# Gate GEMMs as one block of eight pairs with seven block products for eight, other jobs in the SWA stage, GpSimd rotation by tiles

## What is computed

```
h   = RMSNorm(x)
z   = h @ w_in          # q latent 384 | kv latent 256 | rope key 32 | SWA q 512 | SWA k 128 | SWA v 128 | gates 2048
A   = multi-head latent attention, 8 heads, chunk-causal (64-frame chunks)
B   = sliding-window attention, 8 heads on 2 kv heads, this chunk and two before, learned sinks
m   = sum_b sigmoid(gate_b) * (branch_b @ w_branch[b])
x   = x + RMSNorm(m @ w_out)
x   = x + RMSNorm(SwiGLU(RMSNorm(x)))
```

## Time and profile before

| | us |
|---|---|
| median of three runs | 902.55 (902.31 to 903.01) |
| the profiled execution, own time | 903.12 |
| its span, first to last instruction | 901.3 |
| TensorE busy in the span | 885.1 |
| VectorE busy | 491.9 |
| ScalarE busy | 385.4 |
| GpSimd busy | 75.7 |

### The profile page before, as it was taken

The page is one execution under the profiler, slowest core; times in us unless marked ns, Lnnn a source line. Parts: engine busy times, 40 slices in busy tenths (PEclk is TensorE's granted clock), DMA queues, the critical chain, the costliest instruction groups (busy, mean ns, idle before and its releaser), DMA issues.

```text
span 901.3 us, 13817 instructions
## 1 busy us (share of the span) xinstructions
PE 885.1 (98%) x5513; PEld 804.0 (89%) x5513; DVE 491.9 (55%) x758; ACT 385.4 (43%) x769; POOL 75.7 (8%) x73
## 2 busy tenths in 40 slices
PE   8999999999999998999999999999999999999997
PEld 7888999999976877998789999999999998888886
DVE  5523532433354565564779877777777774343124
ACT  5211422335453555452666545444445443332112
POOL 0300197140030000000000000000000000000000
PEclk9999999999999999999999999999999999999999
DMA  7623245153330001654612233332233326222202
GB/s 271 176 78 93 69 128 179 57 158 92 100 71 1 2 1 36 205 181 181 193 72 81 83 93 95 94 87 76 73 94 94 94 84 242 72 72 93 71 24 117
DMA packets 101599, 91.97 MB, mean 102 GB/s; under 512 B 8496, under 2 KB 85312, under 8 KB 101392
## 3 DMA queue, kind: packets, MB, share of 16 engines
q1 hardware_dynamic: 95216, 86.19, 30.9%
q10 hardware_dynamic: 5424, 2.99, 1.1%
q0 software_dynamic: 896, 1.92, 0.7%
HBM read 79.60 MB, written 12.40 MB: 102 GB/s over the span
## 4 chain that ended last, share of the span: by engine, by line
PE 90%; DVE 5%; ACT 4%; issue 1%; DMA 0%; DVEq 0%; POOL 0%; ACTq 0%; POOLq 0%
PE ps L1180 26%; PE ps L1181 25%; PE ps L1182 25%; PE ps L1362 2%; PE ps L1411 1%; PE ps L1373 1%; PE ps L1235 1%; PE ps L1458 1%; PE ps L1332 1%; PE ps L1405 1%; PE ps L1336 1%; ACT probs L897 1%; PE ps L1433 1%; PE ps L1443 1%; DVE nm_c L1735 1%
## 5 line engine op out<-in xcount | busy, mean ns | idle before, releaser
L1671 DVE TENSOR_TENSOR wlo<-raw,whi 128x1024 fp32r<-128x1024 f32 x59 | 79.0, 1342 | 206.0 <-ACT whi L824 198.5
L824 ACT ACTIVATE whi<-raw 128x1024 fp32r<-128x1024 f32 x59 | 62.1, 1056 | 179.3 <-PE ps L1182 167.6
L1180 PE MATMUL ps<-h_hi,wlo 128*128 128x320 f32 x288 | 90.7, 315 | 0.0
L1182 PE MATMUL ps<-h_hi,whi 128*128 128x320 f32 x288 | 89.0, 309 | 0.0
L1181 PE MATMUL ps<-h_lo,whi 128*128 128x320 f32 x288 | 88.9, 309 | 0.0
L1180 PE MATMUL ps<-sc_hi,t_lo 128*128 128x320 f32 x252 | 77.9, 309 | 0.9 <-DVE t_lo L1898 0.9
L1036 ACT ACTIVATE t_hi<-wd 128x512 fp32r<-128x512 f32 x84 | 52.8, 629 | 60.3 <-DVE wd L1952 55.9
L1182 PE MATMUL ps<-sc_hi,t_hi 128*128 128x320 f32 x252 | 77.8, 309 | 0.0
L1181 PE MATMUL ps<-sc_lo,t_hi 128*128 128x320 f32 x252 | 77.8, 309 | 0.0
L1180 PE MATMUL ps<-whi,gu_lo 128*128 128x512 f32 x190 | 74.0, 390 | 0.2 <-DVE gu_lo L2022 0.2
L1181 PE MATMUL ps<-wlo,gu_hi 128*128 128x512 f32 x190 | 73.9, 389 | 0.0
(11 more groups left out here) (308 smaller groups left out, 2143.9 us busy)
## 6 DMA issues: line engine op xcount, KB each, us to landing
raw<-in_w_gate_up SPq DMA_DIRECT2D x44, 512.0 KB, 3.8
raw<-in_w_down SPq DMA_DIRECT2D x22, 512.0 KB, 3.7
raw<-in_w_in SPq DMA_DIRECT2D x16, 512.0 KB, 4.1
raw<-in_w_in SPq DMA_DIRECT2D x12, 480.0 KB, 4.8
gates_scratch<-gate_s SPq DMA_DIRECT2D x16, 320.0 KB, 2.4
gate_r<-gates_scratch SPq DMA_DIRECT2D x8, 640.0 KB, 4.4
raw<-in_w_branch SPq DMA_DIRECT2D x8, 512.0 KB, 5.3
raw<-in_w_out SPq DMA_DIRECT2D x8, 512.0 KB, 6.0
```

What stands on the lines that cost most here:

```text
L824: act.activation(whi[:, r % 2, :] if to is None else to, raw[:, r, :], ACT.Copy).then_inc(w_hi, 1)
L1180: pe.matmul(out, left[1], right[0], start=first, stop=False, skip_group_check=not own_group)
L1182: return pe.matmul(out, left[0], right[0], start=False, stop=last, skip_group_check=not own_group)
L1671: dve.tensor_tensor(lo[:, place, :], raw[:, r, :], hi[:, place, :].bitcast(F32), ALU.subtract).then_inc(w_lo, 1)
```

## The change

The gates' 16 column blocks are computed as eight pairs in one block ahead of the transposes of z (`GATE_PRODUCTS`, `gate_product`). With a pair's weights in quarters and h in quarters, seven products of 4 `mm3` (12 matmuls of 320 columns) stand for eight. The quarter sums of h are made by VectorE between the z slots (`h_add`, `hs_raw`, `part_sum_lo`); differences and splits of the weights (`gate_difference`, `gate_split_hi`, `gate_split_lo`) and the reads of the banks (`gate_read`) are interleaved by product number, five products ahead. SyncE stores both blocks of a pair. The statistics of z (`z_square`) are spread over the products on ScalarE, the normalisation (`z_normalise`) over them on VectorE.

In the SWA stage the gate halves are gone. In their places stand jobs, given by a table: for each chunk, those after the scores, those after the values of the chunk before, and those after the turn. These jobs have two banks in turn.

```
-JOBS1 = 5 * TILES
+JOBS1 = len(TURNS)
+AHEAD = [("uq", 0), ("uq", 1)]
+CHUNK_JOBS = [
+    ([("uq", 2)], [("uq", 3), ("uq", 4)], []),
...
+    ([("wuk", n) for n in range(4)], [("cache", b) for b in range(STREAMS)], []),
+    ([("q", n) for n in range(4)], [("q", n) for n in range(4, 10)], []),
+    ([("v", 0)], [("v", 1), ("qabs", 0)], []),
+    ([("qabs", 1), ("qabs", 2)], [("qabs", 3), ("v", 2)], [("v", 3)]),
+]
 def job_bank(j):
-    return 4 + (j + 3) % 4 if j < JOBS1 else (j - JOBS1) % 4
+    return 4 + (j + 1) % 4 if j < JOBS1 else (j - JOBS1) % 2
...
+GATE_PAIRS = 8
+GATE_PRODUCTS = [("m1", 0), ("m2", 0)]
+for p in range(GATE_PAIRS - 1):
+    GATE_PRODUCTS += [("m5", p), ("m6", p), ("m1", p + 1), ("m7", p), ("m2", p + 1), ("m4", p), ("m3", p)]
+GATE_PRODUCTS += [(kind, GATE_PAIRS - 1) for kind in ("m5", "m6", "m7", "m4", "m3")]
+GATE_BANKS = [(7, 0, 1), (2, 3, 4)]
```

On TensorE:

```
+            def gate_product(n):
+                kind, p = GATE_PRODUCTS[n]
...
+                pe.wait_ge(gp_lo_rdy, n + 1)
+                if kind == "m1":
+                    pe.wait_ge(g_c21, p - 1) if p >= 2 else pe.wait_ge(bank_empty, 10 + 5 * p)
...
+                elif kind == "m3":
+                    pe.wait_ge(g_c22, p + 1)
...
+                for k in range(4):
...
+                    ins = mm3(ps[:, bank, 0:HALF], (gp_hi[kind][:, w], gp_lo[kind][:, w]), right, first and k == 0, k == 3,
+                              first)
+                ins.then_inc(gp_used, 1)
...
+                elif j >= JOBS1 + 2:
+                    job_emptied(pe, j - 2)
...
             for c in range(NCH):
                 chunk_scores(c)
-                pe.wait_ge(w_lo, G1 + c + 1)
-                pe.wait_ge(g_out, 8 + c)
-                wide(c % 2, h_hi, h_lo, (0, 1), 0, 4, KD)
+                for j in chunk_jobs(c, 0):
+                    job(j)
                 if c:
                     chunk_values(c - 1)
-                wide(c % 2, h_hi, h_lo, (0, 1), 4, KD, KD).then_inc(w_used, 1)
+                for j in chunk_jobs(c, 1):
+                    job(j)
                 chunk_turn(c)
+                for j in chunk_jobs(c, 2):
+                    job(j)
+            chunk_values(NCH - 1)
```

On VectorE, the loop of the gate block and the end of a chunk (ScalarE has the same two splits at the end of chunk 1):

```
+            for n in range(NG):
+                gate_read(n)
+                if n + LEAD + 1 < NG and GATE_PRODUCTS[n + LEAD + 1][0] in DIFFERENCES:
+                    gate_difference(*GATE_PRODUCTS[n + LEAD + 1])
+                if n + LEAD < NG:
+                    gate_split_lo(n + LEAD)
+                if 13 <= n < 13 + 4 * TILES and n % 2:
+                    z_normalise((n - 13) // 2)
...
             for c in range(NCH):
                 chunk_max(c)
+                for j in chunk_jobs(c, 0):
+                    job(j)
                 chunk_normalise(c)
                 if c:
                     chunk_out(c - 1)
-                after_slot(G1, 0, c)
+                for part in (1, 2):
+                    for j in chunk_jobs(c, part):
+                        job(j)
+                if c == 1:
+                    split_lo(BRC + 1, 0)
+                    split_lo(BRC + 2, 1)
             chunk_out(NCH - 1)
```

On GpSimd the rotation of z no longer waits for the normalisation, and goes tile by tile, ten operations each, then six for the keys of all tiles; the copy of v and the rotation of q come after the gate block:

```
             pool.wait_ge(bank_empty, 15)
             pool.wait_ge(tab_in, 16 * 4)
-            pool.tensor_copy(v_s[:], z[:, :, C_VS:MIX_COLS]).then_inc(v_s_rdy, 1)
+            for t in range(TILES):
+                rope_products(t)
+                rope_sums(t)
+            key_rope_products()
+            key_rope_sums()
             pool.wait_ge(z_norm, 2 * TILES)
```

More of the change, by code:

```diff
@@ L60, with chunk_jobs @@
 SLOTS = DN0 + KF
[L64 to L69, removed]
-JOBS1 = 5 * TILES
+TURNS = [(kind, t) for t in range(TILES) for kind in ("qlat", "ckv", "qs")]
+JOBS1 = len(TURNS)
+AHEAD = [("uq", 0), ("uq", 1)]
+CHUNK_JOBS = [
+    ([("uq", 2)], [("uq", 3), ("uq", 4)], []),
+    ([("uq", 5)], [("uq", 6), ("uq", 7)], []),
+    ([("uq", 8)], [("uq", 9), ("kt", 0)], []),
+    ([("kt", 1)], [("kt", 2), ("kt", 3)], []),
+    ([("wuk", n) for n in range(4)], [("cache", b) for b in range(STREAMS)], []),
[3 more added lines that the diff above has]
+]
+JOBS = TURNS + AHEAD + [job for chunk in CHUNK_JOBS for part in chunk for job in part]
+def chunk_jobs(c, part):
+    at0 = JOBS1 + len(AHEAD) + sum(len(jobs) for chunk in CHUNK_JOBS[:c] for jobs in chunk)
+    at0 += sum(len(jobs) for jobs in CHUNK_JOBS[c][:part])
+    return range(at0, at0 + len(CHUNK_JOBS[c][part]))
 def job_bank(j):
-    return 4 + (j + 3) % 4 if j < JOBS1 else (j - JOBS1) % 4
+    return 4 + (j + 1) % 4 if j < JOBS1 else (j - JOBS1) % 2
 def job_engine(kind, n):
@@ new lines, in rope_sums @@
+            def rope_sums(t):
+                pairs = z[:, t, C_QS:C_KS].rearrange("p (i g d) -> p i g d", i=4, g=2)
+                keys = z[:, t, C_KS:C_VS].rearrange("p (h d) -> p h d", d=HD)
+                pool.wait_ge(z_rot, ROPE_STEPS * t + 4)
+                for heads, to in ((slice(0, 4), pairs[:, :, 0, :]), (slice(4, 8), pairs[:, :, 1, :]), (slice(8, 10), keys)):
+                    pool.tensor_tensor(to[:, :, 0:32], rope_a[:, heads], rope_b[:, heads], ALU.subtract).then_inc(z_rot, 1)
+                    pool.tensor_tensor(to[:, :, 32:64], rope_c[:, heads], rope_d[:, heads], ALU.add).then_inc(z_rot, 1)
@@ L883, in _, with part_sum_hi @@
-            for i, width in enumerate((QL, KVL)):
+            def part_sum_hi(i):
+                act.wait_ge(hs_sum, i + 1)
+                act.activation(hs_hi[:, i], hs_raw[:, i], ACT.Copy).then_inc(hs_hi_rdy, 1)
+            for j in range(6):
+                after_slot(4, 0, j)
+                if j == 2:
+                    part_sum_hi(0)
+                elif j == 3:
+                    part_sum_hi(1)
+                elif j == 4:
+                    part_sum_hi(2)
+                    part_sum_hi(3)
```

506 lines of the change are left out of this document (340 added, 166 removed).

## The result

The changed kernel takes 908.17 us (median of 4 runs, 907.99 to 908.63), the kernel before beside it 902.43 us: a ratio of 1.0064, interval 1.0049 to 1.0079. It is slower by 0.6%, with 96 matmuls fewer. The forecast was 903.4, with 895.0 to 911.5 as its range and a chance of 0.38 for slower.

What follows compares the result with a forecast made beforehand. TensorE's queue length plus its waits was taken as the bound. The profiled 903.1 - 14.1 + 2.6 + 12.35 gave 904.0, and 903.4 after allowing for that run standing 0.6 over the median; range 895 to 911.5.

Steps and rivals of the forecast that it cites:

- forecast case: Whole kernel: the prediction's main case, a time of 900 to 907 us, chance 0.45.
- rival A: Gate block: VectorE and GpSimd operations alternate at full length without overlap, 16 us of TensorE waiting, 916.8 us; chance 0.22.
- Gate blocks, -14.1: Gate matmuls on TensorE: 96 fewer of 320 columns at 0.147 us each, 14.1 us removed.
- New work before the block, 0: Before the gate block: 12 added VectorE operations, 17.8 us, fit into its free time from 44 to 97; cost 0.
- VectorE in the gate block, +2.6: Gate block: VectorE, alternating with GpSimd's rotation of z, lags 5.3 us; less 2.7 slack, TensorE waits 2.6 us.
- the slack of 2.7 us: Gate block: m3 needs VectorE's read of m7 with two products between, so 2.7 us of lag was counted as harmless.
- The weighing of the port rule: Gate block: skill's whole-instruction wait set against the trace's 0.3 us overlap per turn; without overlap the sum is 13 us larger.
- Signs for A and B: Gate block length: 101 us by the forecast, 99 by B, over 106 by A, with waits only in the first 50.
- SWA stage, +12.35: SWA stage: TensorE waits, chunk 4 +5.0, chunk 5 +3.6, chunk 2 +1.75, chunk 7 +0.7, first chunk +0.2, end +1.1.
- Rival B: SWA stage: waits for the jobs' two banks do not bite, chunks 4 and 5 cost 1.2 together, 893.4 us; chance 0.24.
- The clock: Whole kernel: waits are only one or two microseconds, so the granted clock was assumed to keep its level; no cost.
- Rival C: SWA stage, chunk 4: cache rows or rotated q arrive 3 us late, 906 us, or the clock falls; chance 0.09.

## Why the prediction was right or wrong

The range held the time, and the sign was the one with the largest chance (0.38). The forecast of no change did not hold: 0.64% is well over the 0.2%, and 908.2 lies above the 900 to 907 of the forecast case. The range held it because it reached halfway into rival A. Two errors also offset each other in part: the gate block's sum was 6.7 us too low, the SWA stage's 1.7 too high. By steps:

- *Gate blocks, -14.1.* Right. Without waits the products run at 0.147 us, and the block with an empty rotation lasts 100.2, the forecast 98.6 and 1.5 for its last pair.
- *New work before the block, 0.* Right: no new stop between 26 and 95 us.
- *VectorE in the gate block, +2.6.* This is the step that failed: it measured 9.3 us (107.9 against 98.6), the mis-sized term of the sum. The turn was right: a low part and a 320-element product start every 1.28 us where 0.69 + 0.87 - 0.3 makes 1.26. The lag was right too: 5.3 us forecast (2.5 from the start, 2.8 from two pairs with normalisations), and TensorE's stops there are 2.5 at the entry and 3.1 at 131 and 135. What failed is the slack of 2.7 us that I took off. It is the time between VectorE's read of m7 and m3, and none of the stops was for that, nor for a low part, the two waits that I had named. All of them, at the entry, at 131 and 135 and in the last pair, were for ScalarE's reads of a bank. Ahead of the last pair these reads stood in ScalarE's queue behind a cast that waits for VectorE (at 106 also behind two squares of z's statistics), a path that the sum does not have. Two terms were not in the sum at all: the stops of the last pair, 1.5, and the half clock behind the 2.5 us stop, 1.5. 5.6 + 1.5 + 1.5 are 8.6 of the 9.3.
- *The weighing of the port rule.* The Trainium skill, "SBUF — State Buffer", section "Who interferes with whom", has the loser wait for the whole instruction. In this trace the two hand over a little sooner, 1.28 us a turn against 1.56, the two durations together (0.69 + 0.87). The size of the turn was not where I went wrong, so the full-turn reasoning of rival A is not what happened either, though its time, halfway (910), is nearer than mine. The section also says that a VectorE operation with at most one input in SBUF does not contend, and the trace agrees: VectorE's reads of a bank take 0.48 to 0.49 in the middle of the rotation.
- *Signs for A and B.* I had set 106 us for the block as A's mark, with waits in the first 50 us and not after. It was 107.9, with 4.8 us of idle time in the first 51 and 1.2 in the last pair. So A's mark was passed without A's full turns: a length alone did not tell a longer turn from slack that was not there.
- *SWA stage, +12.35.* Near: from the first transpose of z to the MLA stage the two kernels differ by 10.7 us beyond the eight gate slots. Chunk 4 lost 4.6 (5.0 forecast), chunk 5 3.3 (3.6), chunk 2 1.4 (1.75, from 9.02 against 7.56 to 7.60 with the splits elsewhere), chunk 7 0.5 (0.7), the end 1.4 (1.1). Idle time 8.9, within the bounds of 6 and 18. Rival B fell: the waits for a job's bank are there (view of chunk 4), though no run with four banks says what they would cost.
- *The clock.* "I assume the level stays" failed, at one place in the changed kernel. I had named a fall of it as a sign that I was wrong, and had given it no price.
- *Rival C.* No wait names a DMA; q's rotation ends at 244.3, and the first job that needs it starts at 249.8.

## What to carry to other kernels

Where an engine feeds another through a third, count the lag along each queue, not only along the data: a read whose bank is full stood behind a cast whose data was not there, and the slack of the data's own path did not help. Work on GpSimd was not free beside VectorE's operations with two inputs in SBUF, and its price was set per turn: what decided was whether VectorE's operations plus one of GpSimd's for each still fit into TensorE's time for that stretch. So smaller operations on GpSimd, the same work on VectorE itself, or the other work of VectorE moved out of the stretch can each win. The stop of 2.5 us cost another 1.5 behind it, at the lower clock, so look at the granted clock in windows of 2 us behind each.

## What the runs showed that I had not expected

- VectorE and GpSimd take turns, one operation each, for as long as both have operations that read SBUF (VectorE with two inputs there): 1.36 us for a 512-element subtraction beside 320-element products, 1.02 beside 160, 0.95 beside 128, 0.80 beside 64, 0.69 alone. The same rotation in 76 instead of 56 operations made the kernel 5.9 us faster (902.27 against 908.17).
- The granted clock fell to half behind the stop of 2.5 us, in all five kernels whose profile has that stop, and in other kernels behind two waits of 1.3 and 0.8 us (the other table of jobs) or 0.7 and 1.0 in a stretch of transposes (the later normalisations, the rotation on VectorE); behind the same waits of 0.66 and 1.01 in chunk 4 it did not fall in the changed kernel. It stayed down for 3 to 9 us. What decides was not tested.
- The rest of a program, untouched, varies by 1.4 us at its start and 1.7 at its end between profiled executions. With differences of a microsecond only the stage itself can be compared, not the total.
